# Plain FFN up-projection: the 512-column and the 256-column product of each tile in alternation instead of sorted by length

## The reference, cut to what matters

```
def swiglu(x, w13, w2):                     # x 256 x 1024, w13 1024 x 5632, w2 2816 x 1024
    gate, up = jnp.split(x @ w13, 2, axis=-1)
    return (jax.nn.silu(gate) * up) @ w2

x = layer_norm(ALPHA * x + 0.5 * swiglu(x, ffn1_w13[i], ffn1_w2[i]), ln_g[i, 0], ln_b[i, 0])
```

## Time and profile before

| | us |
|---|---|
| median of 3 runs | 2730.32 (2729.82 to 2733.73) |
| the profiled execution: span | 2727.5 |
| TensorE busy (matmul) | 2651.0, 97% |
| GpSimd busy | 1972.7, 72% |
| ScalarE busy | 1386.9, 51% |
| VectorE busy | 1017.6, 37% |

### The profile page before, as it was taken

One profiled execution on the slowest core, in us unless ns is written; L12 is line 12 of the kernel. 1 busy time (PEld: TensorE's weight loads), 2 busy tenths in 40 slices (PEclk: granted clock), 3 DMA queues, 4 the chain that ended last, 5 costly groups with the idle time before them and its releaser, 6 DMA issues.

```text
span 2727.5 us, 35975 instructions
## 1 busy us (share of the span) xinstructions
PE 2651.0 (97%) x15016; PEld 2269.8 (83%) x15016; DVE 1017.6 (37%) x1695; ACT 1386.9 (51%) x1666; POOL 1972.7 (72%) x432
## 2 busy tenths in 40 slices
PE   6999989999999999999999999999999999999998
PEld 4889977899888778888888888888888888877887
DVE  6868867543212452121124311212441121244312
ACT  3754544555544555454454544544544454445543
POOL 3767764787887738878875688887658878774885
PEclk8999989999999999999999999999999999999999
DMA  8869843555554526546553455554425555443553
GB/s 331 309 230 353 311 157 108 191 213 182 200 193 175 181 88 223 188 170 216 186 197 137 160 186 194 192 192 177 155 111 199 192 193 192 179 179 115 194 192 108
DMA packets 80390, 521.78 MB, mean 191 GB/s; under 512 B 8908, under 2 KB 9292, under 8 KB 24420
## 3 DMA queue, kind: packets, MB, share of 16 engines
q1 hardware_dynamic: 72884, 492.72, 49.9%
q10 hardware_dynamic: 7344, 26.74, 2.5%
HBM read 518.38 MB, written 1.05 MB: 190 GB/s over the span
## 4 chain that ended last, share of the span: by engine, by line
PE 89%; DVE 6%; ACT 2%; DMA 1%; issue 0%; POOL 0%; SPq 0%; DVEq 0%; ACTq 0%
PE acc L555 17%; PE acc L594 17%; PE mb L532 11%; PE cb L532 11%; PE cb L507 10%; PE cb L534 6%; PE mb L534 6%; PE mb L647 2%; PE acc L872 1%; DVE hT L1875 1%; PE acc L507 1%; PE cb L833 1%; PE mb L857 1%; PE cb L647 1%; ACT whi L1184 1%; DMA raw<-in_w 1%
## 5 line engine op out<-in xcount | busy, mean ns | idle before, releaser
L2512 POOL TENSOR_TENSOR wlo<-raw,whi 128x2048 fp32r<-128x2048 f32 x428 | 1972.5, 4621 | 731.4 <-ACT whi L1184 667.3
L1184 ACT ACTIVATE whi<-raw 128x2048 fp32r<-128x2048 f32 x428 | 818.4, 1915 | 582.5 <-PE cb L532 251.3
L555 PE MATMUL acc<-whi,ARR 128*128 128x512 f32 x1312 | 366.5, 391 | 0.0
L532 PE MATMUL cb<-hT,whi 128*128 128x512 f32 x1280 | 335.4, 393 | 0.0
L532 PE MATMUL mb<-hT,whi 128*128 128x512 f32 x1280 | 334.1, 393 | 0.1
L555 PEld LDWEIGHTS acc<-whi,ARR 128*128 128x128 f32 x1312 | 245.6, 188 | 53.0 <-issue 2.9
L507 PE MATMUL cb<-hT,whi 128*128 128x256 f32 x1536 | 281.1, 285 | 0.0
L594 PE MATMUL acc<-whi,hT 128*128 128x512 f32 x960 | 270.8, 390 | 8.7 <-DVE hT L1875 7.4
L532 PEld LDWEIGHTS mb<-hT,whi 128*128 128x128 f32 x1280 | 230.2, 189 | 43.9 <-issue 3.1
L532 PEld LDWEIGHTS cb<-hT,whi 128*128 128x128 f32 x1280 | 229.6, 189 | 40.5
L1944 DVE TENSOR_TENSOR cb<-cb,AR 128x512 f32<-128x512 f32 x80 | 56.0, 700 | 552.8 <-ACT AR L1192 552.7
(11 more groups left out here) (332 smaller groups left out, 3367.6 us busy)
## 6 DMA issues: line engine op xcount, KB each, us to landing
raw<-in_w SPq DMA_DIRECT2D x436, 1024.0 KB, 4.8
AR<-in_a ACTq DMA_DIRECT2D x35, 512.0 KB, 6.2
AR<-in_a SPq DMA_DIRECT2D x29, 512.0 KB, 5.7
z<-in_a ACTq DMA_DIRECT2D x16, 512.0 KB, 6.8
gb<-in_lng SPq DMA_DIRECT2D x12, 512.0 KB, 5.7
gb<-in_lnb SPq DMA_DIRECT2D x12, 512.0 KB, 6.5
gb<-in_normg SPq DMA_DIRECT2D x8, 512.0 KB, 7.6
x<-in_x SPq DMA_DIRECT2D x1, 1024.0 KB, 8.4
```

What stands on the lines that cost most here:

```text
L532: ins = pe.matmul(to[j], wh[:, w], hT[:, k, :], start=k == 0, stop=k == 7)
L555: ins = pe.matmul(acc[:, 2 * t + c, 0:c1 - c0], xs[y], a[:, kk * width + c0:kk * width + c1], start=first and kk == 0 and m == 0, stop=las ...
L1184: ac.activation(whi[i % NH][:, :], raw[u % NR][:, :], ACT.Copy).then_inc(*up(s_hi, ("hi", i)))
L2512: po.tensor_tensor(wlo[i % NH][:, :], raw[(i + NADA) % NR][:, :], whi[i % NH][:, :].bitcast(F32), ALU.subtract).then_inc(*up(s_lo, ("lo", i)))
```

## The change

The order of the 16 matmuls of a half is another. Before it is (True, 0), then (False, 0) to (False, 7), then (True, 1) to (True, 7). After it is (True, 0), (False, 0), (True, 1), (False, 1), and so on to (True, 6), (False, 6), and at the end (False, 7), (True, 7). The bank is opened and closed by the same products.

```diff
-            ORDER = [(True, 0)] + [(False, k) for k in range(8)] + [(True, k) for k in range(1, 8)]
+            ORDER = [(both, k) for k in range(7) for both in (True, False)] + [(False, 7), (True, 7)]
```

## The result

Alternation made the kernel slower: 2738.71 us (median of 5 runs, 2735.67 to 2741.64) against 2730.32 (2728.37 to 2733.73), a ratio of 1.0031 with a 95% interval of 1.0018 to 1.0043. The forecast was 2726.8. The profiled execution has a span of 2733.9 us, 6.4 more than before; TensorE is busy for 7 us longer, the other engines as long as before.

What follows compares the result with a forecast made beforehand. TensorE's issue of matmuls was taken as the bound; 2.784 - 2.795 = -0.011 us per half, x 320 = -3.5 us, so 2730.3 - 3.5 = 2726.8 us. Range 2712 to 2742.

Steps and rivals of the forecast that it cites:

- What bounds, and where: Plain FFN: TensorE's issue of matmuls bounds, busy 97% of the span; L532 and L534 are 34% of the chain.
- Price before: Split unit: a half of 16 matmuls costs 2.795 us, settled prices 2.773 plus 0.02 per round trip of lengths.
- Price after: Alternating half: 0.230 us per 512 plus 0.118 per 256, 0.348 per pair, eight pairs 2.784 us.
- The bound above: Alternating pair, dear end: 0.233 to 0.236 for a 512 behind a shorter matmul, pair up to 0.356, +17 us.
- break-even: Alternating pair: at 0.3494 us per pair (2.795 / 8) the change neither gains nor loses time.
- The second: L532 behind L534: every 512 pays first settling steps again, 0.353 to 0.356 per pair, +9 to +17 us; chance 0.27.
- The fourth: Alternating halves: order has no effect but for the settling that goes, 0.3467 per pair, -7 us; chance 0.12.
- The first: Alternating pairs: every 256 starts early behind a 512, 512s stay settled, 0.340 per pair, -24 us; chance 0.18.
- the third: Alternating pairs: alternation hides the 256s' 0.013 us wait on loads, 0.333 per pair, -41 us; chance 0.03.
- the nearest row: L594, 512 and 160 columns in turn: seven pairs in 2.40 us, 0.343 per pair.
- The exclusion: Alternating halves: the whole 0.02 us round trip at every pair (45 us) is excluded, as L594 loses only 0.006 per pair.
- the forecast's own range: Kernel time 2724 to 2733 us, from 0.347 to 0.3505 per pair, -6 to +3 us; chance 0.40.

Runs made afterwards that it cites:

- e1: Against the kernel before: both halves of a split unit share one round trip of lengths (fourteen 512s, sixteen 256s, two 512s); 0.9993 of before (0.9983 to 1.0002).
- e10: Against the sorted kernel before: all plain FFN stages alternate 512 and 256 across the two banks; median 0.25 us above, gate units 5.643 us, value units 5.550.
- e9: Untimed, order per stage: gate units enter alternation with three, four or five 512s behind four 256s; 346.7, 346.7, 353.3 ns per pair; other stages seek the cheapest period, 16.560 us.
- e4: Untimed, against the alternating kernel: the short matmul has 128 to 448 columns, one width per stage; with 128 alternating units were cheaper than sorted, with 448 alternation cost most.
- e6: Untimed: split units start with one to eight 512s by stage, then alternate across banks; value units 346.7 ns per pair with leads 1 and 2, all others 353.3.
- e3: Untimed: eight orders of the same 32 matmuls, one per plain FFN stage, including runs of two to four, another group k, other banks; another k changed nothing.
- e8: Untimed alternating controls: all 512 columns, high weights alone, exchanged weights, short widths 240 to 272; all-512 units 7.253 us, high-alone and exchanged 5.643 gate, 5.550 value.
- e5: Untimed, in the sorted order of before: the short matmul has 128 to 448 columns, one width per stage; 384-column matmuls in a row went at 171 to 186 ns.

## Why the prediction was wrong, by its steps

**What bounds, and where.** Right: no idle time, clock and chain as before, no other engine late, and no other line's start-to-start sum moved by more than 2 us. L532's rose by 12.0 us and L534's fell by 5.2. L555's 24 matmuls, which were to stay at 5.44, took 5.447.

**Price before.** Right: 2.795 per half by rounded starts, 2.793 by ns; the settled prices 226.7 and 120.0 were confirmed in every run, and the 0.02 us per round trip by e1.

**Price after: the step that failed.** "I take 0.230 for the 512 [...] and 0.118 for the 256". The 256 was 0.1167 (113, 117, 120 in turn). The 512 was 0.2367 (233, 241, 236). The 0.230 was a mean over eight or nine neighbouring 512s, most of which don't stand behind a shorter matmul: in the run of eight the first two take 233 and 236 ns and the last ones 227. The bound above, 0.233 to 0.236, was the nearer price, and I rated it lower. It was no better founded: no row is given for its 0.236, and its 0.233 is 0.343 less an assumed 0.11, where the trace of before has distances of some 270 ns behind the 512 and 74 behind the 160. Nor would single distances have done: a T directly behind an f was 233 there and an f directly behind a T 113, together 0.346, under break-even. The 241 of the dear rhythm stands nowhere in the sorted order. The step that failed is thus to take a matmul's price from its length and its neighbour's, whatever stood before them. With 0.3533 per pair for 0.348, eight pairs give 2.826 for 2.784, and the half, with its 256s and 512s that adjoin at the end, had 2.818: +8.0 us for -3.5.

**The rivals.** The second had the sign, the place and the size, 0.353 per pair, +9 us. That is in part luck. Its mechanism was wrong: I priced it as settling paid anew at each change, and runs of two, e10 and e9 show that there is no such price. Its two terms, 0.233 and 0.120, were both off (0.2367 and 0.1167) and made up for each other. The fourth, 0.3467, is what the same alternation does from another entry. The first (0.340) and the third (0.333) occurred nowhere: no steady pair of 512 and 256 columns came below 346 ns. The Trainium skill, "TensorE: Matmul & The Clock Gate", section "Back-to-back issue gap", has a formula for a matmul by itself; by an estimate from it the pair would be 325 ns, and no order of this stream came near that.

**The exclusion.** That the whole 0.02 of a round trip isn't paid per pair was right (0.007 is), though the rows that I drew it from belong to widths with rhythms of their own, and the 0.006 rests on the same assumed 0.11.

**The chances and the range.** The range held the time, but the forecast's own range, 2724 to 2733, did not, and the sign was wrong. More than 0.27 for slower could be argued from the nearest row, an alternation itself; but e4 has alternation at other widths from 0.022 us per unit cheaper than sorted to 0.075 dearer, and no row of before could tell 0.3467 from 0.3533.

**What stays open.** Why these rhythms exist. Banks (e6), group k (e3), weight values and buffers (e8) don't decide. The work of other engines beside TensorE was not varied; that a sequence repeats to 2 or 3 ns in all eight instances of a stage speaks against it but doesn't exclude it. Something that works in steps of 16 cycles and carries state over some matmuls would fit the 6.67 ns quantum, but no run shows what it is.

## What to carry to other kernels

When matmuls of two lengths stand next to each other and TensorE is the bound, their order can be worth some ns per matmul, and neither the number of changes nor the length of the runs tells which order is good: put several orders into the stages of one kernel and read the distance from start to start in one trace. For an order that isn't in the trace, a mean over a run is the wrong price for a matmul that stands alone between others; a row nearer in kind gives a guess and no more, since the same alternation cost 346.7 or 353.3 ns by its entry (e9) and other widths have other excesses (e4). Give both signs a fair chance, and look at a whole period, because a unit's tail is paid by the next (the down-projection unit took 5.447 us behind alternation and 5.440 behind the sorted order).

## What the runs showed of the hardware that was not expected

At the full clock the distance between matmul starts settles at columns / 2.4 + 13.3 ns for 256, 320 and 512 columns alike (120.0, 147, 226.7), with fp32r operands and a new weight tile each time. Behind a long run of the other length the first ones deviate in a fixed order (T 233, 236, 228, 232, 231, 227 ns; f 113, 119, 120), the same to 1 ns in all instances of the sorted order. An alternation of 512 and 256 has at least three steady rhythms. In the gate units of e9, behind four 256s, three 512s led to 346.7 ns per pair with a period of one pair, four to 346.7 with a period of two, and five to 353.3 with a period of three. For other widths the sequence need not settle to one distance (384 columns: 171 to 186 ns in a row of eight). Fewer columns can take longer: in the sorted order (e5) a unit with 128-column short products took 5.495 us and one with 192-column ones 5.440; the first 512 behind them took 282 to 292 ns with 128 columns and 252 with 192, which the first short product (57 to 60 and 86 ns) gave back only in part.
